# Rounding the odd channel tiles of a norm on GpSimd instead of ScalarE

## What is computed

```python
def rms_norm(x, w):
    xf = x.astype(jnp.float32)
    y = xf * lax.rsqrt(jnp.mean(xf * xf, axis=-1, keepdims=True) + EPS)
    return (y * w.astype(jnp.float32)).astype(x.dtype)

def modulate(h, shift, scale):
    return h * (1 + scale) + shift
...
        xl = xl + 0.5 * ml[2] * swiglu(modulate(rms_norm(xl, norm_ffn1[l]), ml[0], ml[1]), ffn1_w13[l], ffn1_w2[l])
...
        h_lat = modulate(rms_norm(xl, norm_mix[l]), ml[3], ml[4])
...
        xl = xl + ml[5] * (mix_l @ w_out[l])
        xl = xl + 0.5 * ml[8] * swiglu(modulate(rms_norm(xl, norm_ffn2[l]), ml[6], ml[7]), ffn2_w13[l], ffn2_w2[l])
```

## Time and profile before

| | |
|---|---|
| Median of 3 runs | 1918.3 us (1915.81 to 1920.09) |
| The profiled execution's own time | 1920.51 us |
| Its span, first to last instruction | 1918.8 us |
| TensorE busy (matmul) | 1807.6 us, 94% |
| VectorE busy | 1411.3 us, 74% |
| ScalarE busy | 734.3 us, 38% |
| GpSimd busy | 51.6 us, 3% |
| Mean granted TensorE clock | 0.959 of full speed |

### The profile page before, as it was taken

The page is one execution under the profiler, slowest core; times in us unless marked ns, Lnnn a source line. Parts: engine busy times, 40 slices in busy tenths (PEclk is TensorE's granted clock), DMA queues, the critical chain, the costliest instruction groups (busy, mean ns, idle before and its releaser), DMA issues.

```text
span 1918.8 us, 25690 instructions
## 1 busy us (share of the span) xinstructions
PE 1807.6 (94%) x9154; PEld 1477.6 (77%) x9154; DVE 1411.3 (74%) x2310; ACT 734.3 (38%) x1075; POOL 51.6 (3%) x101
## 2 busy tenths in 40 slices
PE   8999999978998898999999989999998899879999
PEld 5788888866775576788888768888886677569999
DVE  6877878778777657877878658787775878656766
ACT  4322222245656545222222352222224655654342
POOL 1000000000000000000000000000000000000000
PEclk8899999999999898999999989999998899789999
DMA  8444353413212043444444223534430322024443
GB/s 360 175 154 174 137 186 136 176 42 141 78 59 96 1 154 113 181 166 153 175 153 153 110 88 133 186 141 174 154 133 22 132 94 110 23 110 176 175 175 110
DMA packets 37583, 259.44 MB, mean 135 GB/s; under 512 B 4369, under 2 KB 5841, under 8 KB 7441
## 3 DMA queue, kind: packets, MB, share of 16 engines
q1 hardware_dynamic: 26066, 182.32, 25.8%
q0 software_dynamic: 11456, 76.32, 10.8%
HBM read 252.60 MB, written 5.24 MB: 134 GB/s over the span
## 4 chain that ended last, share of the span: by engine, by line
PE 82%; ACT 8%; DVE 6%; issue 2%; DMA 1%; SPq 0%; DVEq 0%; ACTq 0%
PE ps L1412 24%; PE ps L1413 24%; PE ps L1414 24%; ACT n_t L572 2%; PE ps L1477 2%; DVE mod_prod L890 1%; PE ps L1685 1%; PE ps L1747 1%; DVE x_res L971 1%; ACT w_hi L528 1%; PE ps L1650 1%; ACT h_hi L575 1%; ACT w_hi L535 1%; DVE w_lo L872 1%; PE ps L1660 1%
## 5 line engine op out<-in xcount | busy, mean ns | idle before, releaser
L1412 PE MATMUL ps<-h_hi,w_hi 128*128 128x512 f32 (+1 forms) x1872 | 693.6, 371 | 42.6 <-DVE h_lo L942 31.9
L1413 PE MATMUL ps<-h_lo,w_hi 128*128 128x512 f32 (+1 forms) x1872 | 687.7, 367 | 0.0
L1414 PE MATMUL ps<-h_hi,w_lo 128*128 128x512 f32 (+1 forms) x1872 | 687.0, 367 | 0.0
L1412 PEld LDWEIGHTS ps<-h_hi,w_hi 128*128 128x128 f32 x1872 | 358.8, 192 | 112.1 <-issue 36.2
L1414 PEld LDWEIGHTS ps<-h_hi,w_lo 128*128 128x128 f32 x1872 | 358.4, 191 | 58.4
L1413 PEld LDWEIGHTS ps<-h_lo,w_hi 128*128 128x128 f32 x1872 | 358.7, 192 | 57.0 <-issue 0.2
L971 DVE SCALAR_TENSOR_TENSOR x_res<-ps,abg,x_res 128x256 f32<-128x256 f32 x640 | 272.0, 477 | 157.2 <-PE ps L1414 156.4
L867 DVE TENSOR_TENSOR w_lo<-raw,w_hi 128x2048 fp32r<-128x2048 f32 x132 | 301.9, 2287 | 98.4 <-ACT w_hi L528 98.4
L528 ACT ACTIVATE w_hi<-raw 128x2048 fp32r<-128x2048 f32 x132 | 252.2, 1912 | 272.7 <-PE ps L1414 266.4
L890 DVE CUSTOM_DVE_ANT_0 mod_prod<-mod_raw,cb 128x1024 f32<-128x1024 f32 x256 | 301.5, 1218 | 1.6 <-ACT cb L688 1.5
L1412 PE MATMUL ps<-a_hi,w_hi 128*128 128x512 f32 (+1 forms) x640 | 233.4, 365 | 5.7 <-DVE x_res L971 5.7
(11 more groups left out here) (215 smaller groups left out, 1410.9 us busy)
## 6 DMA issues: line engine op xcount, KB each, us to landing
raw<-ffn_in SPq DMA_DIRECT2D x132, 1024.0 KB, 4.8
mod_raw<-mod_in POOLq DMA_DIRECT2D x68, 1024.0 KB, 5.1
raw<-proj_in SPq DMA_DIRECT2D x20, 1024.0 KB, 4.8
raw<-out_w_in SPq DMA_DIRECT2D x8, 1024.0 KB, 6.4
x_spill<-x_res SPq DMA_DIRECT2D x2, 2048.0 KB, 7.9
x_res<-x_spill SPq DMA_DIRECT2D x2, 2048.0 KB, 7.7
x_res<-x_in SPq DMA_DIRECT2D x2, 1024.0 KB, 12.4
scale_w<-scale_in POOLq DMA_DIRECT2D x4, 512.0 KB, 11.4
```

The lines of the kernel that those rows point to most:

```text
L1412: pe.matmul(dst, w_hi[:, slot, wsl], hi, start=first, stop=False)
L1413: pe.matmul(dst, w_hi[:, slot, wsl], lo, start=False, stop=False)
L1414: return pe.matmul(dst, w_lo[:, slot, wsl], hi, start=False, stop=last)
```

## The change

ScalarE's rounding of a norm's tile is skipped for odd `d` in norms 1 to 5; GpSimd does it with a `tensor_copy` from `n_t` into `h_hi`, behind the same wait for the affine step, and counts it on a semaphore of its own, `h_hi_odd`. VectorE's `remainder` waits for that semaphore for odd tiles. Norm 0 is as it was.

```diff
+        h_hi_odd = sem("h_hi_odd")
...
+            def round_odd(n, nt):
+                for d in range(1, KT, 2):
+                    pool.wait_ge(aff_done, AFF_BASE[n] + len(streams(nt)) * (d + 1))
+                    pool.tensor_copy(h_hi[:, d, 0:nt], n_t[:, d % 2, 0:nt]).then_inc(h_hi_odd, 1)
...
                 load_stretches(f)
+                if f < 3:
+                    round_odd(*NORM_AFTER[f])
                 if f % 2 == 0:
                     mixer_rows(f // 2)
+                    round_odd(3 * (f // 2) + 2, out_tokens(f // 2))
...
                     act.wait_ge(aff_done, AFF_BASE[n] + len(streams(nt)) * (d + 1))
-                    act.activation(h_hi[:, d, 0:nt], n_t[:, d % 2, 0:nt], ACT.Copy).then_inc(h_hi_s, 1)
+                    if n == 0 or d % 2 == 0:
+                        act.activation(h_hi[:, d, 0:nt], n_t[:, d % 2, 0:nt], ACT.Copy).then_inc(h_hi_s, 1)
...
                 def remainder(d):
-                    dve.wait_ge(h_hi_s, 8 * n + d + 1)
+                    if d % 2:
+                        dve.wait_ge(h_hi_odd, 4 * (n - 1) + d // 2 + 1)
+                    else:
+                        dve.wait_ge(h_hi_s, 4 * (n + 1) + d // 2 + 1)
```

## The result

| | before | after |
|---|---|---|
| Median | 1918.2 us (1915.52 to 1920.65, 6 runs) | 1924.7 us (1923.37 to 1925.65, 6 runs) |
| Profiled execution, its span | 1920.5, 1918.8 us | 1924.4, 1922.5 us |
| ScalarE, GpSimd busy | 734.3, 51.6 us | 725.2, 71.9 us |
| Mean granted clock | 0.959 | 0.961 |

The changed kernel is **slower**: ratio 1.0035, 95% interval 1.0022 to 1.0047, 6.5 us. The forecast was 14.2 us more. The direction and the place of the largest loss were right, the size was less than half.

What follows compares the result with a forecast made beforehand. TensorE, holding 82% of the chain, was taken to bound the kernel. Terms 1.7 + 8.4 + 1.9 + 1.0 + 1.2 = 14.2 us on the profiled 1920.5 gave 1934.7, or a median of 1932.5 us; range 1921 to 1941.

Steps and rivals of the forecast that it cites:

- Norm 1: First mixer: copies delay VectorE, tile 7's copy starts after the weight split, last subtraction at 441.75 instead of 440.05; +1.7 us.
- Norm 2, late product: Into the second FFN: piece 14's load queues behind tile 7's copy, VectorE's first product 5.5 us late, all reaching TensorE.
- Norm 2, clock: Behind norm 2: TensorE's standstill grows to 6.8 us, then half speed at clock 0.50; 2.9 us lost.
- Norm 3: Into the third FFN: two splits of 2.29 us around tile 7, the first without a copy behind it; +1.9 us.
- Norm 4: Second mixer: last multiply, which the spill waits for, is late; TensorE's later standstill hides the norm's own delay; +1.0 us.
- Norm 5: Norm of 256 columns with 0.5 us copies, estimated at 0.7 of norm 1; +1.2 us.
- ScalarE's relief: In the norms: taking roundings from ScalarE gains at most 0.08 us per two tiles, 0.3 us a norm.
- The late end of the range for a copy's start: GpSimd's copy starts only when VectorE's running instruction ends, not when the affine step ends.
- VectorE's four passes and the copy stand in one line: Within a norm, from tile 1 on: two tiles take 3.54 us instead of 3.30, +0.24 per pair.
- B: Rival: no exclusion and a copy as fast as the memset, so not slower; +0.8 us, 1919.1 us; chance 0.10.
- C: Rival: exclusion and a slow copy of 1.2 us, each copy adding 0.45 us; 1940.5 us; chance 0.15.
- A: Rival: no exclusion, copy of 0.75 us, VectorE 2.9 us late for piece 14; 1924.7 us; chance 0.15.

Runs made afterwards that it cites:

- e5: Changed kernel with piece 14's load ahead of norm 2's copies and each norm's last late weight split behind tile 7's subtraction: 1911.9 us, ratio 0.9964.
- e1: Kernel before, all roundings on ScalarE, only the loads of pieces 14 and 15 made to wait for norm 2's last subtraction: 1922.7 us, ratio 1.0031.
- e2: Changed kernel with the load of piece 14 issued ahead of norm 2's copies, piece 15 still behind them: 1918.0 us, ratio 0.9999.
- e4: Kernel before with only the last late weight split of each norm moved behind tile 7's subtraction: 1910.2 us, ratio 0.9959.
- e9: Kernel before with both the first and the last late weight splits moved behind tile 7's subtraction: 1913.2 us, ratio 0.9979.
- e10: Kernel before with every late 2.29 us split behind tile 7's subtraction, the small split of norms 1 and 4 left in place: 1909.9 us, ratio 0.9965.
- e0: Kernel before, unchanged, run again for a second profile: 1915.4 us, ratio 0.9994.
- e7: Kernel before, unchanged, run once more beside the later runs: 1917.2 us, ratio 0.9997.
- e8: Kernel before with the last late split behind tile 7's subtraction, run a second time: 1910.2 us, ratio 0.9972.

## Why the prediction was right and wrong

| Term | forecast | measured in its stretch |
|---|---|---|
| Norm 1 | +1.7 | +0.7 |
| Norm 2, late product | +5.5 | +5.8 |
| Norm 2, clock | +2.9 | +1.8 |
| Norm 3 | +1.9 | +0.9 |
| Norm 4 | +1.0 | 0.0 |
| Norm 5 | +1.2 | +0.4 |
| Sum | +14.2 | +9.6 |

The forecast was 7.7 us too high for the median. Of these the terms above account for 4.6: the norms were 3.8 too dear and the clock 1.1, and the late product was 0.3 too cheap. The other 3.1 lie between the sum of the stretches and the medians and stay open.

**Right.** No gain from ScalarE's relief: it was busy 9.1 us less, and none of the six stretches got shorter. The late end of the range for a copy's start (it waits for VectorE's running instruction), shown by e5. The load of piece 14 behind tile 7's copy as the main loss, shown alone by e1 and undone by e2. VectorE's first product was 751.72 - 731.93 = 19.79 us behind tile 0 where it had been 14.05, so 5.7 late against 5.5. That fit is partly luck, as two errors cancelled: the issue came 12.5 us behind tile 0 (744.39 - 731.93) where I had 13.6 (747.45 - 733.85), and the first half landed in 7.1 us where I took 6.0. The standstill of 6.3 (6.8 forecast) and the clock of 0.50 behind it came as described.

**Wrong: the price of a copy, and what it stands behind.** The step that failed is that from tile 1 on "VectorE's four passes and the copy stand in one line", 3.54 us for two tiles, so that the norm would run 0.80 late into the split. The pair took 3.33. I had the copy at 0.75 from VectorE's end; a waiting copy ends 0.46 to 0.48 after the row it waited for, under my lower end of 0.53, as if a row outlasted its hold on the other engine by 0.14 (0.62 - 0.48, an estimate). With it VectorE's line is 0.72 + 0.69 + 0.03 + 0.48 + 0.03 + 0.72 + 0.60 = 3.27, and the odd tile's own chain is what binds: multiply 0.69, affine 1.09, copy 0.62, subtraction 0.69 and four hand-overs of 0.24 in all, 3.33. I had those hand-overs at 0.12. (One reading was off as well: before tile 6 VectorE had idled 0.16, at 437.24, not 0.23.) So the exclusion bites twice in a norm, at its first copy (0.25) and at the last. In norm 1 the split started 9.75 us behind TensorE's tile 0 where it had been 9.68, so 0.07 late instead of 0.80, and tile 7's copy behind the split cost 0.59 instead of 0.90. TensorE's idle time before tile 7 grew by 0.60, not by 1.5 to 2. The same over-sizing made norm 3, and with 256 columns norm 5, where the last copy outlasted the split by 0.27:

```profile
1731.56 2.15 POOL L477 CAST h_hi<-n_t 128x256 fp32r<-128x256 f32 x1 [1.68 <-ACT n_t L581]
```

```profile
1731.16 2.28 DVE L877 TENSOR_TENSOR w_lo<-raw,w_hi 128x2048 fp32r<-128x2048 f32 x1
```

**Norm 4** went for the same reason: the spill waits for the last multiply, which was 0.3 late instead of 1.03, and the spill itself took 8.31 us instead of 8.61, which by itself gives the 0.3 back.

**The clock.** This term was mis-sized too. I took the 6.1 us at half level of the earlier trace rows, after a standstill of 4.33; here it was 3.9 (to 784.3) after 6.33, in e1 5.7 (to 787.7) after 6.89. How long the level stays down is not a function of the standstill in these three rows, and a term taken from one such row missed here by 1.1 us.

**The rivals.** B and C are out: the copy is neither without exclusion nor 1.2 us. A named a time, 1924.7, that is the median to the tenth, by a mechanism that did not occur: it had the loads only 2.9 us late and the norms nearly free. A time alone tells no mechanism; the 6.55 us of VectorE's stall and the 2.03 of the last copy do.

**What stays open.** The stretches say +9.6, the medians +6.5. In every edited kernel the difference of the medians lies 1.3 to 4.8 us below that of the stretches, slower and faster ones alike (e1 4.4 for 8.5, e4 -8.4 for -3.6, e9 -2.9 for -1.1, e10 -7.8 for -4.7); for the two repeats of the unchanged kernel it lies 5.4 below (e0, -2.8 for +2.6) and 1.1 above (e7). So part is chance: the medians of one kernel scatter by 3 us, and a stretch too can differ with the clock, as e0's from norm 3 to norm 4 did (378.7 for 376.2). That it always has the same sign in the edited kernels is not explained. Whether the mixers' clock also depends on the schedule before them is left open by e8 and was not tried by itself.

## What to carry to other kernels

Before work is given to an idle engine, read what is queued behind the new place on that engine: here a DMA issue with 50 us of lead lost it, and that was three quarters of the loss in the stretches. A GpSimd copy is cheap beside VectorE instructions of its own length and dear behind a long one; and where TensorE waits for the tile behind a long instruction that nobody needs yet, moving that instruction behind the tile can gain what an engine swap does not: 4.7 us in the stretches of e10, where the swap lost 9.6. When one is moved, look for other queues that wait for it, as the spill did for the small split.

## What was not expected of the hardware

- A GpSimd copy of 128x512 from fp32 to fp32r takes 0.62 us by itself (norm 1, and e5 with VectorE idle), 0.41 for 256 columns (norm 5): as fast as ScalarE's 0.63 and VectorE's 0.69, nearly as fast as a memset of 0.53 that reads nothing.
- A waiting copy's row starts when its semaphore releases it (438.75, 0.06 after the affine step's end) and includes the wait, so its length (2.03, 2.15) says nothing of the copy; its end does. The Trainium skill (SBUF — State Buffer, section Who interferes with whom) calls the shared port pair an exclusive lock, and says of VectorE's two-port modes that whoever issues first has the pair for the whole instruction. The trace shows the same for a `tensor_tensor` with two inputs: the waiting copy ended 0.48 us after a split of 2.28.
- The granted clock of the second mixer's rest was 0.89 in one profile of the kernel before and 0.92 in another, 199.75 and 194.37 us for the same instructions: a single profile can't tell a change of under 5 us there.
